# Two expert weight pieces loaded into the upper half of the gate buffer, before the output products of a hybrid decoder layer

## The chip, the cores and the metric

The kernel runs on one core of one Trainium2 chip. The metric is the device time of one execution in microseconds. TensorE is PE in the rows, VectorE DVE, ScalarE ACT, GpSimd POOL, and SyncE, which issues most of the transfers, SP.

## What is computed

One step of a one-layer hybrid decoder: 512 prompt tokens and 64 sample tokens, 1024 channels. A state-space branch and a sparse attention branch each give 1024 channels. They are multiplied by gates, added, multiplied by `w_out` and added to the input. Behind that stands a mixture of experts with 32 experts in 4 groups, two experts for a token. Cut to what matters here:

```python
gates = sigmoid(g_mrg)                      # 2 x 1024 channels, one half for each branch
merged = gate_ssm * ssm_out + gate_attn * attn_out
x = x + merged @ w_out
h = rms_norm(x, g_ffn)
g_sel = argmax(h @ w_router_group + b_router_group)
top_v, top_i = top_k(e_logits[g_sel], 2)    # h @ w_router_expert + b_router_expert
for block, e in blocks_of_tokens_by_expert:
    out[block] = (silu(h[block] @ w_exp_gate[e]) * (h[block] @ w_exp_up[e])) @ w_exp_down[e]
y = rms_norm(x + weighted sum of a token's two rows of out, g_final)
```

## The kernel before, in words

Everything is float32. The program is written by hand, engine by engine, with semaphores; no scheduler moves anything. It has five phases, and the last, `tail`, joins `merge` (branches, output product, router), `experts` and `combine`. Each engine runs its three parts one behind the other.

**The buffers.** `c.arena` is one tensor of on-chip memory that the phases cut up again and again with `Region`. In `merge`, `sig` (line 1565) holds 16 tiles of 128 channels by 576 tokens from `AT_Z4` on: tiles 0 to 7 are the gates of the state-space branch, tiles 8 to 15 those of the attention branch. Behind `sig` lie `g_ffn`, `w_route`, `b_route`, and the row buffer `X_rows` with its tables. The attention products are multiplied into tiles 8 to 15 (line 1881). The state-space products are multiplied into tiles 0 to 7 (line 1909), and tiles 8 to 15 are added to them (line 1910, semaphore `proj_done`, 16 steps). The output product (line 1779) reads tiles 0 to 7 alone, so tiles 8 to 15 are dead from `proj_done` 16 on.

**The weights of the experts.** An expert has six pieces of 1 MB (`w_exp[b, p]`): four of gate and up weights, two of down weights. `c.sets` (line 1595) has three sets of six places, all of them over buffers of `merge` that are dead by the time. Expert b uses set b modulo 3. Set 1's pieces 2 to 5 lie over `sig`, as does set 2's piece 4, which also reaches into `g_ffn`.

**The order of the transfers.** SP issues them in the order of the program, and waits block all that stands behind:

```python
        sp.wait_ge(proj_ps, 16)
        for s, p in ((0, 3), (0, 4), (0, 5), (1, 0), (1, 1)):
            piece(s, p)
        for i in range(TILES - 1):
            sp.wait_ge(h_ready, i + 1)
            sp.dma_start(c.d["h"][...], h[...]).then_inc(h_stored, 16)
            sp.wait_ge(h_stored, 16 * (i + 1))
        sp.wait_ge(out_ps, 2 * TILES)
        for s, p in ((1, 2), (1, 3), (1, 4), (1, 5), (2, 0), (2, 1), (2, 2), (2, 3)):
            piece(s, p)
        sp.wait_ge(h_ready, TILES)
        piece(2, 4)
```

Behind it, in `experts`, line 2108 refills a place when TensorE has used its piece (`gu_used`, line 2107, and `down_used`, line 2112). The last piece of expert 2, line 2119, waits until the router's tables and weights are done.

**Router and first rows.** DVE forms h tile by tile (`normed`, line 1928, `h_ready`), SP writes it to memory (line 1668), and POOL writes the last tile (line 1682). PE turns h over (line 1761) and forms the logits with `w_route` (line 1769); DVE chooses the experts (`choose`, line 1931 on; the last mask, line 1965, is `m_ready`). PE ranks the tokens (lines 1798 to 1801), DVE and PE find the tokens of the first two experts (lines 1992 and 1808), and POOL gathers their rows of h from memory into `X_rows` by two indirect transfers (line 1688). PE begins expert 0 with the transposes of the gathered rows (line 2186), then gate and up products (line 2199, each half gives back two places), then the full tables (line 1816), for which DVE has worked in the meantime (lines 2019 to 2031).

Of the kernel before, what the change touches and what calls it, by code (L numbers as in the profile page):

```python
# [28 lines left out]
P = 128  # L29
# [4 lines left out]
TOK = SEQ + NB * NT  # L34
HALF = TOK // 2
TILES = 5
# [132 lines left out]
AT_Z4 = 4992  # L169
# [1386 lines left out]
def merge(nc, c):  # L1556


    def sem(name):
        return c.sem("merge_" + name)  # L1560
# [3 lines left out]
    small = Region(c.arena, AT_Z4 + 16 * TOK, AT_KT)  # L1564
# [14 lines left out]
    g_ffn = small.take([P, D])  # L1579
    w_route = small.take([P, KD, 36])  # L1580
    b_route = small.take([P, 36])
    c.X_rows = small.take([SLOTS, 2, D])
    c.table = small.take([SLOTS, TABLE, 2], I32)
    c.blocks = small.take([1, BLOCKS + 3], I32)
    c.token = small.take([SLOTS, 2, 1], I32)
    at_z = Region(c.arena, AT_Z4, AT_Z4 + 5 * 2048)
    at_out = Region(c.arena, AT_KT, AT_XM)
    at_attn = Region(c.arena, AT_X2_END, AT_LOCAL)
    at_glu = Region(local, 3072, 3072 + 6 * 2048)
    over_z = [at_z.take([P, 4, 512]) for _ in range(5)]  # L1590
    over_out = [at_out.take([P, 4, 512]) for _ in range(4)]
    over_attn = [at_attn.take([P, 4, 512]) for _ in range(2)]
    over_glu = [at_glu.take([P, 4, 512]) for _ in range(6)]
    over_w1 = Region(c.arena, c.w1_at, c.w1_at + 2048).take([P, 4, 512])
    c.sets = [[over_w1] + over_attn + over_glu[0:3], over_glu[3:5] + over_z[0:4], over_out + [over_z[4], over_glu[5]]]

    ss = route.take([P, TILES])
    lg = route.take([P, TILES, 36])
# [23 lines left out]
    glu_ps, glu_tanh, glu_done, proj_ps, proj_done, out_ps, x_done = (  # L1622
        sem("glu_ps"), sem("glu_tanh"), sem("glu_done"), sem("proj_ps"), sem("proj_done"), sem("out_ps"),
        sem("x_done"))
    sq2, h_ready, h_stored, ht_ps, ht_out, lg_ps = (
        sem("sq2"), sem("h_ready"), sem("h_stored"), sem("ht_ps"), sem("ht_out"), sem("lg_ps"))
    ge_ready, ge_exp, te_ready, te_exp, m_ready, rank_ps, pick_ready, table_ps = (
        sem("ge_ready"), sem("ge_exp"), sem("te_ready"), sem("te_exp"), sem("m_ready"), sem("rank_ps"),
        sem("pick_ready"), sem("table_ps"))
# [13 lines left out]
    def sync(sp):  # L1643
        sp.dma_start(w_attn[:], c.d["w_attn"]).then_inc(wa_in, 16)
        sp.dma_start(sig[:, 8:16], c.d["sig"][8:16].rearrange("m p t -> p m t")).then_inc(gate_a_in, 16)
        sp.dma_start(w_glu[:], c.d["w_glu"]).then_inc(wg_in, 16)
        sp.dma_start(w_ssm[:], c.d["w_ssm"]).then_inc(ws_in, 16)
        sp.dma_start(sig[:, 0:8], c.d["sig"][0:8].rearrange("m p t -> p m t")).then_inc(sig_in, 16)
        sp.dma_start(g_ffn[:], c.d["g_ffn"]).then_inc(rt_in, 16)
        sp.dma_start(w_route[:], c.d["w_route"]).then_inc(rt_in, 16)  # L1650
        sp.dma_start(b_route[:], c.d["b_route"]).then_inc(rt_in, 16)
        def piece(s, p):
            sp.dma_start(c.sets[s][p], c.d["w_exp"][s, p]).then_inc(c.piece_in[s][p], 16)

        piece(0, 0)
        sp.wait_ge(y_ps, NY)
        sp.dma_start(w_out[:], c.d["w_out"]).then_inc(wo_in, 16)
        sp.wait_ge(attn_ps, 16)
        sp.dma_start(x[:, 0:4], c.d["x"][0:SEQ].rearrange("(i p) d -> p i d", p=P)).then_inc(x_in, 16)
        sp.dma_start(x[0:64, 4], c.d["x"][SEQ:TOK]).then_inc(x_in, 16)  # L1660
        piece(0, 1)
        piece(0, 2)
        sp.wait_ge(proj_ps, 16)
        for s, p in ((0, 3), (0, 4), (0, 5), (1, 0), (1, 1)):
            piece(s, p)
        for i in range(TILES - 1):
            sp.wait_ge(h_ready, i + 1)
            sp.dma_start(c.d["h"][i * P:i * P + ROWS[i]], h[0:ROWS[i], i % 2]).then_inc(h_stored, 16)
            sp.wait_ge(h_stored, 16 * (i + 1))
        sp.wait_ge(out_ps, 2 * TILES)  # L1670
        for s, p in ((1, 2), (1, 3), (1, 4), (1, 5), (2, 0), (2, 1), (2, 2), (2, 3)):
            piece(s, p)
        sp.wait_ge(h_ready, TILES)
        piece(2, 4)

    def gpsimd(pool):
# [190 lines left out]
    def vector(dve):  # L1867
# [188 lines left out]
        dve.wait_ge(c.weights_ready, 1)  # L2056

    return sync, gpsimd, tensor, table_tensor, scalar, vector


# [318 lines left out]
def tail(nc, c):  # L2379

    with ExitStack() as ctx:
        c.tail_local = local_tensor(nc, ctx, "tail")
        merge_sync, merge_gpsimd, merge_tensor, table_tensor, merge_scalar, merge_vector = merge(nc, c)
        experts_sync, experts_gpsimd, experts_tensor, experts_scalar, experts_vector = experts(nc, c, table_tensor)
        combine_sync, combine_scalar, combine_vector = combine(nc, c)
# [192 lines left out]
```

## Time and profile before

| | us |
|---|---|
| median of 3 runs | 1260.64 (1260.14 to 1262.17) |
| the profiled execution, its own time | 1264.99 |
| its span | 1263.3 |
| busy in the span: PE | 1041.9 |
| busy in the span: DVE | 410.2 |
| busy in the span: ACT | 328.0 |
| busy in the span: POOL | 251.9 |

Busy time of an engine is the time in which it has an instruction under way. The profiled execution is 4.35 us above the median, and its span, from the first to the last instruction, is 1.7 us shorter than its own time. Transfers are busy by 16 engines that all queues share, and their share is the mean over these. Times in the trace are counted from the start of the span.

### The profile page before, as it was taken

The numbers are of one execution on the slowest core, as the hardware profiler recorded it, in microseconds if no ns is written. First come the engines' busy times: TensorE is split into PE (matmuls) and PEld (weight loads), VectorE is DVE, ScalarE is ACT, GpSimd is POOL, SyncE is SP. The second block draws the span as 40 slices with busy tenths as digits, with TensorE's granted clock in tenths as the row PEclk, the third lists the DMA queues.
The fourth block names the chain that finished last, engine by engine and source line by source line (L and its number), as shares of the span: only waits on it lengthen the run. The fifth ranks groups of instructions, "written<-read, shape, count | busy, mean of one in ns | idle before, by whom it ended". The sixth has DMA issues, their size and how long they took to land.

```text
span 1263.3 us, 17373 instructions
## 1 busy us (share of the span) xinstructions
PE 1041.9 (82%) x6707; PEld 662.2 (52%) x6707; DVE 410.2 (32%) x917; ACT 328.0 (26%) x666; POOL 251.9 (20%) x551
## 2 busy tenths in 40 slices
PE   5999999779987776989999589987877788888870
PEld 5999999656665553767644333333332333333320
DVE  4346536646844443422413520100000000000006
ACT  6432221445642222120011112322222122211222
POOL 0005960388832110000000001111110111111010
PEclk9999999887978887989999679999899999998895
DMA  8322334331017542770220869999999999999956
GB/s 341 138 68 70 108 120 163 104 149 34 2 38 255 181 134 90 315 275 1 76 123 17 322 254 402 390 401 415 403 405 398 406 402 403 405 407 410 405 228 229
DMA packets 74993, 299.64 MB, mean 237 GB/s; under 512 B 12471, under 2 KB 34871, under 8 KB 48407
## 3 DMA queue, kind: packets, MB, share of 16 engines
q1 hardware_dynamic: 65854, 279.89, 57.5%
q0 software_dynamic: 7904, 17.59, 4.3%
q8 instruction: 53, 0.87, 0.3%
q10 hardware_dynamic: 1152, 1.05, 0.3%
q14 instruction: 30, 0.24, 0.1%
HBM read 284.26 MB, written 25.05 MB: 245 GB/s over the span
## 4 chain that ended last, share of the span: by engine, by line
DMA 27%; PE 25%; DVE 3%; issue 2%; SPq 2%; ACT 1%; POOL 0%; POOLq 0%
DMA local_tail<-in_w_exp 14%; DMA arena<-in_w_exp 11%; PE ps L2199 6%; PE ps L1779 5%; PE ps L1739 3%; PE ps L1700 3%; PE ps L1749 2%; PE ps L2216 2%; SPq L2108 1%; PE ps L2186 1%; PE ps L1716 1%; DVE arena L2358 1%; PE ps L1711 1%; SPq L2113 1%; DMA arena<-scratch_h,arena 1%
## 5 line engine op out<-in xcount | busy, mean ns | idle before, releaser
L352 PE MATMUL ps<-local_project 128*128 128x288 f32 (+4 forms) x1608 | 207.2, 291 | 15.3 <-DVE local_project L490 11.6
L2199 PE MATMUL ps<-arena,local_tail 128*64 128x512 f32 x760 | 196.7, 607 | 27.7 <-DMA arena<-in_w_exp 20.3
L352 PEld LDWEIGHTS ps<-local_project 128*128 128x128 f32 (+1 forms) x1608 | 205.8, 185 | 16.3 <-DVE local_project L391 11.5
L2301 DVE SCALAR_TENSOR_TENSOR local_tail<-arena,ps 64x512 f32<-64x512 f32 x32 | 21.7, 679 | 427.4 <-ACT arena L2267 427.4
L2199 PEld LDWEIGHTS ps<-arena,local_tail 128*64 128x64 f32 x760 | 63.2, 139 | 133.7 <-issue 132.1
L2216 PE MATMUL ps<-arena 128*64 128x512 f32 x256 | 89.3, 679 | 32.4 <-DMA arena<-in_w_exp 15.6
L2144 POOL DMA_INDIRECT scratch_rows<-local_tail,arena x32 | 29.5, 922 | 394.3 <-ACT local_tail L2275 393.2
L2216 PE MATMUL ps<-local_tail,arena 128*64 128x512 f32 x256 | 89.6, 681 | 16.1 <-DMA local_tail<-in_w_exp 16.1
L2199 PE MATMUL ps<-local_tail 128*64 128x512 f32 x264 | 80.1, 596 | 5.3 <-DMA local_tail<-in_w_exp 4.2
L2275 ACT ACTIVATE local_tail<-ps 64x512 f32<-64x512 f32 x64 | 37.9, 593 | 148.4 <-PE ps L2216 147.6
L2216 PEld LDWEIGHTS ps<-arena 128*64 128x64 f32 x256 | 26.4, 155 | 76.9 <-issue 73.5
L1779 PE MATMUL ps<-arena 128*128 128x512 f32 x128 | 57.4, 609 | 1.0 <-DVE arena L1910 1.0
L391 DVE TENSOR_TENSOR local_project<-arena,local_project 128x2048 fp32r<-128x2048 f32 (+1 forms) x15 | 35.6, 2372 | 66.6 <-ACT local_project L302 66.6
L2267 ACT ACTIVATE arena<-ps 64x512 f32<-64x512 f32 x32 | 18.9, 592 | 131.8 <-PE ps L2199 131.8
L2216 PEld LDWEIGHTS ps<-local_tail,arena 128*64 128x64 f32 x256 | 26.6, 155 | 39.4 <-issue 39.2
L2186 PEld LDWEIGHTS ps<-arena 64*128 64x128 f32 x297 | 24.7, 159 | 34.3 <-issue 26.0
L1269 PE MATMUL ps<-local_attention,arena 128*128 128x128 f32 x256 | 34.6, 298 | 9.0 <-DMA local_attention<-in_cache 7.5
L1779 PEld LDWEIGHTS ps<-arena 128*128 128x128 f32 x128 | 24.7, 195 | 31.8 <-issue 30.3
L2263 ACT ACTIVATE arena<-ps 128x256 f32<-128x256 f32 x32 | 12.3, 384 | 110.3 <-PE ps L2186 110.2
L2199 PEld LDWEIGHTS ps<-local_tail 128*64 128x64 f32 x264 | 24.7, 136 | 29.6 <-issue 28.1
L1269 PEld LDWEIGHTS ps<-local_attention,arena 128*128 128x128 f32 x256 | 33.0, 211 | 10.1 <-DMA local_attention<-in_cache 7.9
L2140 POOL DMA_INDIRECT arena<-scratch_h,arena x32 | 30.0, 938 | 30.7 <-DVE arena L2035 20.8
(401 smaller groups left out, 1505.7 us busy)
## 6 DMA issues: line engine op xcount, KB each, us to landing
arena<-in_w_exp SPq DMA_DIRECT2D x127, 1024.0 KB, 29.0
local_tail<-in_w_exp SPq DMA_DIRECT2D x65, 1024.0 KB, 29.4
arena<-in_w_rest SPq DMA_DIRECT2D x9, 1024.0 KB, 5.6
local_attention<-in_cache SPq DMA_DIRECT2D x56, 128.0 KB, 2.7
arena<-in_w_wide SPq DMA_DIRECT2D x6, 1040.0 KB, 4.9
arena<-scratch_sig SPq DMA_DIRECT2D x2, 2304.0 KB, 13.4
arena<-in_x SPq DMA_DIRECT2D x2, 2048.0 KB, 11.7
arena<-in_cache SPq DMA_DIRECT2D x32, 128.0 KB, 2.2
```

Source lines behind the costliest of these rows:

```text
L352: mm = pe.matmul(out, stationary(s, k), moving(m, k), start=k == 0 and a == 0, stop=k == KD - 1 and a == 2)
L391: dve.tensor_tensor(W[:, n % 2, 1, :, 0:width], raw[:, n % 2, :, 0:width], W[:, n % 2, 0, :, 0:width].bitcast(F32), ALU.subtract).then_inc ...
L1269: mm = pe.matmul(c.ps[:, 5, quarter * P:(quarter + 1) * P], c.w1[:, s, j], mov, start=j == 0, stop=j == 7)
L1700: mm = pe.matmul(c.ps[:, 6 + u % 2, 0:HALF], w_attn[:, k, m * P:(m + 1) * P], c.aT[:, k, t], start=k == 0, stop=k == 3)
L1739: mm = pe.matmul(c.ps[:, 2 * e + u % 2, 0:HALF], w_glu[:, k, (4 * e + j) * P:(4 * e + j + 1) * P], yT[:, k, t], start=k == 0, stop=k == 3)
L1779: mm = pe.matmul(c.ps[:, n, :], sig[:, k, i * P:(i + 1) * P], w_out[:, k, n * 512:(n + 1) * 512], start=k == 0, stop=k == KD - 1)
L2140: pool.indirect_dma_start(X[:, q], None, c.d["h"], bass.IndirectOffsetOnAxis(ap=at.bitcast(U32), axis=0), bounds_check=TOK - 1, oob_is_err ...
L2144: pool.indirect_dma_start(c.d["rows"], bass.IndirectOffsetOnAxis(ap=at.bitcast(U32), axis=0), Y[:, q], None, bounds_check=2 * TOK - 1, oob ...
L2186: return pe.transpose(out, rows, ident) if k else pe.matmul(out, rows, ident, start=True, stop=True)
L2199: mm = pe.matmul(c.ps[SLOTS * u:SLOTS * (u + 1), BANKS[q][u], :], XT[:, 4 * half + k], c.sets[s][2 * half + u][:, k], start=half == 0 and ...
L2216: mm = pe.matmul(c.ps[SLOTS * h:SLOTS * (h + 1), 6 + h, :], HT[:, k], c.sets[s][4 + h][:, k], start=k == 0, stop=k == KE - 1)
L2275: act.activation(Y[:, q, h * 512:(h + 1) * 512], c.ps[SLOTS * h:SLOTS * (h + 1), 6 + h, :], ACT.Copy).then_inc(y_out, 1)
```

## The change

Two pieces of the second expert's weights (set 1, pieces 2 and 3) get places over tiles 8 to 15 of `sig`, and SP issues them when `proj_done` stands at 16, ahead of the stores of h. Pieces 4 and 5 of set 1 now lie over tiles 0 to 7 and still wait for the output product. Set 2's piece 4 now reaches over `w_route` and `b_route` too, and waits for `m_ready` in place of the fifth `h_ready`. `X_rows` and what lies behind it move up by 188 floats (from 15556 to 15744).

```diff
@@ merge, places
     b_route = small.take([P, 36])
+    at_half = AT_Z4 + 8 * TOK
+    at_tail = at_half + 2 * 2048
+    small.pos = max(small.pos, at_tail + 2048)
     c.X_rows = small.take([SLOTS, 2, D])
...
-    at_z = Region(c.arena, AT_Z4, AT_Z4 + 5 * 2048)
+    at_low, at_high = Region(c.arena, AT_Z4, at_half), Region(c.arena, at_half, at_tail + 2048)
...
-    over_z = [at_z.take([P, 4, 512]) for _ in range(5)]
+    over_low = [at_low.take([P, 4, 512]) for _ in range(2)]
+    over_high = [at_high.take([P, 4, 512]) for _ in range(3)]
...
-    c.sets = [[over_w1] + over_attn + over_glu[0:3], over_glu[3:5] + over_z[0:4], over_out + [over_z[4], over_glu[5]]]
+    c.sets = [[over_w1] + over_attn + over_glu[0:3], over_glu[3:5] + over_high[0:2] + over_low, over_out + [over_high[2], over_glu[5]]]
@@ merge, sync
         for s, p in ((0, 3), (0, 4), (0, 5), (1, 0), (1, 1)):
             piece(s, p)
+        sp.wait_ge(proj_done, 16)
+        piece(1, 2)
+        piece(1, 3)
         for i in range(TILES - 1):
...
         sp.wait_ge(out_ps, 2 * TILES)
-        for s, p in ((1, 2), (1, 3), (1, 4), (1, 5), (2, 0), (2, 1), (2, 2), (2, 3)):
+        for s, p in ((1, 4), (1, 5), (2, 0), (2, 1), (2, 2), (2, 3)):
             piece(s, p)
-        sp.wait_ge(h_ready, TILES)
+        sp.wait_ge(m_ready, 1)
         piece(2, 4)
```

The order of SP's transfers around the change, before. Row 421 is the first of the five pieces that wait for `proj_ps`, rows 423 and 424 are the stores of h, and rows 425 to 427 the nine pieces behind the output product. The names of semaphores are those of their first user in the program, since they are used again.

```order
421 L1653 DMA local_tail<-in_w_exp 128x2048 [waits project_chan_tanh]
422 L1653 DMA local_tail<-in_w_exp 128x2048 x4
423 L1668 DMA scratch_h<-local_tail 128x1024 [waits project_mean_ready]
424 L1668 DMA scratch_h<-local_tail 128x1024 [waits project_mean_ready,project_root_done] x3
425 L1653 DMA arena<-in_w_exp 128x2048 [waits project_roped,project_root_done]
426 L1653 DMA arena<-in_w_exp 128x2048 x7
427 L1653 DMA arena<-in_w_exp 128x2048 [waits project_mean_ready]
428 L2108 DMA arena<-in_w_exp 128x2048 [waits experts_gu_used] x3
```

And now:

```order
421 L1657 DMA local_tail<-in_w_exp 128x2048 [waits project_chan_tanh]
422 L1657 DMA local_tail<-in_w_exp 128x2048 x4
423 L1657 DMA arena<-in_w_exp 128x2048 [waits project_gates_tanh]
424 L1657 DMA arena<-in_w_exp 128x2048
425 L1675 DMA scratch_h<-local_tail 128x1024 [waits project_mean_ready]
426 L1675 DMA scratch_h<-local_tail 128x1024 [waits project_mean_ready,project_root_done] x3
427 L1657 DMA arena<-in_w_exp 128x2048 [waits project_roped,project_root_done]
428 L1657 DMA arena<-in_w_exp 128x2048 x5
429 L1657 DMA arena<-in_w_exp 128x2048 [waits sample_ot_out]
430 L2115 DMA arena<-in_w_exp 128x2048 [waits experts_gu_used] x3
```

Two of the eight pieces behind the output product moved ahead of the four stores of h, with a wait of their own, and the ninth piece has another wait. Nothing else in SP's order and nothing in the order of PE, DVE, ACT and POOL is different.

## Rows read from the trace of the kernel before

**Rows 1.** The page: the chain that ended last, by engine and by line.
```profile
DMA 27%; PE 25%; DVE 3%; issue 2%; SPq 2%; ACT 1%; POOL 0%; POOLq 0%
DMA local_tail<-in_w_exp 14%; DMA arena<-in_w_exp 11%; PE ps L2199 6%; PE ps L1779 5%; PE ps L1739 3%; PE ps L1700 3%; PE ps L1749 2%; PE ps L2216 2%; SPq L2108 1%; PE ps L2186 1%; PE ps L1716 1%; DVE arena L2358 1%; PE ps L1711 1%; SPq L2113 1%; DMA arena<-scratch_h,arena 1%
```
**Rows 2.** Windows; behind the stretch: busy us by engine, granted clock, DMA share, GB/s.
```profile
core 0: us, PE busy (x) PEld busy (x) DVE busy (x) ACT busy (x) POOL busy (x), PEclk, DMA share, GB/s
702.00:728.00 26.00, 8.68 (x62) 7.79 (x60) 18.03 (x64) 3.72 (x8) 2.76 (x4) 0.56 0.97 384
728.00:738.00 10.00, 8.55 (x31) 3.42 (x33) 1.20 (x3) 0.60 (x1) 0.00 (x0) 0.60 0.00 1
738.00:748.00 10.00, 9.23 (x57) 4.17 (x53) 3.83 (x17) 1.78 (x3) 1.86 (x2) 1.00 1.01 398
...
760.00:1200.00 440.00, 363.95 (x1761) 143.68 (x1759) 38.12 (x56) 95.62 (x172) 52.94 (x57) 0.95 1.02 404
```
**Rows 3.** Timeline of SP: start, us until the last issue ended, line, count.
```profile
624.31 2.59 SPq L1653 DMA_DIRECT2D local_tail<-in_w_exp  x5
644.29 50.18 SPq L1668 DMA_DIRECT2D scratch_h<-local_tail  x4
701.44 5.41 SPq L1653 DMA_DIRECT2D arena<-in_w_exp  x9
737.09 3.76 SPq L2108 DMA_DIRECT2D arena<-in_w_exp  x3
...
748.01 0.33 SPq L2119 DMA_DIRECT2D local_tail<-in_w_exp  x1
```
**Rows 4.** The chain that ended last, in order of time, 720 to 744 us.
```profile
720.73 7.99 DMA arena<-scratch_h,arena
...
728.76 1.45 PE ps L2186 x9
...
730.88 9.61 PE ps L2199 x32
740.50 0.80 PE ps L2186 x9
741.29 2.37 PE ps L1816 x20
```
**Rows 5.** Windows of 1 us at the end of the nine pieces.
```profile
726.00:727.00 1.00, 0.00 (x0) 0.00 (x0) 0.93 (x3) 0.00 (x0) 0.00 (x0) 0.50 0.92 283
727.00:728.00 1.00, 0.00 (x0) 0.00 (x0) 0.90 (x4) 0.00 (x0) 0.00 (x0) 0.50 0.46 127
```
**Rows 6.** DMA issues (x, us to landing): second gather (722 to 724), loop's last (1205 to 1215); a window.
```profile
arena<-scratch_h,arena POOLq DMA_INDIRECT x1, 6.3
...
arena<-scratch_h,arena POOLq DMA_INDIRECT x1, 6.1
...
1212.50:1215.00 2.50, 2.07 (x13) 0.89 (x11) 0.00 (x0) 0.38 (x1) 0.00 (x0) 1.00 0.72 293
```
**Rows 7.** The last scatter, in the chain; its window; DMA issues of all gathers, 760 to 1200.
```profile
1230.84 3.10 DMA scratch_rows<-local_tail,arena
...
1230.00:1232.50 2.50, 0.00 (x0) 0.00 (x0) 0.00 (x0) 0.02 (x1) 1.44 (x4) 0.69 0.10 23
...
arena<-scratch_h,arena POOLq DMA_INDIRECT x28, 8.0
```
**Rows 8.** Windows of 5 us during and behind the five pieces.
```profile
630.00:635.00 5.00, 5.00 (x13) 2.22 (x12) 0.69 (x1) 0.00 (x0) 0.00 (x0) 1.00 1.01 421
...
640.00:645.00 5.00, 5.00 (x13) 2.28 (x12) 1.65 (x4) 2.64 (x4) 0.00 (x0) 1.00 0.00 0
```
**Rows 9.** Timeline of DVE: the last gated sum, the last mask, the last step before the tables.
```profile
624.81 0.46 DVE L1910 TENSOR_TENSOR arena<-arena 128x288 f32<-128x288 f32 x1
...
714.97 0.26 DVE L1965 TENSOR_TENSOR local_tail<-local_tail 128x96 f32<-128x96 f32 x1
...
728.77 0.49 DVE L2031 TENSOR_TENSOR local_tail<-arena,local_tail 128x320 f32<-128x320 f32 x1
```

## The prediction

> **What bounds the kernel now.** I read the page's chain first. Waits for expert weights are 25% of the span [rows 1], so the long stage of the experts is bound by transfers, not by TensorE. The windows date it: from 738 us to 1200 us the DMA engines show a share of 1.01 or 1.02, at 398 GB/s at its beginning and 404 behind it [rows 2]. A stage like that ends earlier by as much as it starts earlier, or by the bytes that are taken out of it. Here no byte is taken out. The same windows show that the moved pieces belong to an earlier burst: it runs from 702 to 728 us (share 0.97), and then the engines rest for 10 us, share 0.00, until 738. All three sets are full by then, and SP has nothing to issue until TensorE gives back the first place, at 737.09 [rows 3]. So moving 2.10 MB out of the burst does not of itself bring the saturated stage forward. It only makes the rest longer, unless something in the chain waits for the burst.
>
> Something does. The chain in order of time [rows 4] shows what leads to 737.09. When DVE has found the first expert's tokens, POOL issues the gather of their rows, at 720.73, in the middle of the burst, and it takes 7.99 us to land. PE begins at 728.76, ACT copies, and the gate and up products start at 730.88; half of them give back the first place. The gather lands about 0.7 us after the burst is over: the traffic falls to 283 and 127 GB/s in the windows from 726 and 727 us [rows 5], and to nothing behind 728 [rows 2]. The second gather, issued 2.02 us later, takes 6.3 us [rows 6] and so lands at 729.05, 0.33 us after the first. Two requests 2 us apart that land together are held by a common thing, and the weights are what is there.
>
> **The change part by part.**
>
> *The two early pieces.* The five pieces before them are issued by 626.9 [rows 3], and `proj_done` reaches 16 at 625.27 (624.81 and 0.46 [rows 9]), so SP's new wait costs nothing; two more issues at 0.52 us each (2.59 for five) end near 628. At 421 GB/s [rows 8] five pieces of 1.05 MB take 12.5 us, to some 637.5, and two more 5.0, to some 642.5. The next on SP's queue is the first store of h, at 644.29 [rows 3], so it is not held. If it were, by a us or two, ACT needs that store only for the tile two further on, and the tiles are 17 us apart (four stores over 50.18 us [rows 3]). The output products go on meanwhile. Thirteen records in each 5 us with the engines at 421 GB/s, and thirteen with them at rest [rows 8]: weights that arrive cost PE nothing. Price 0.
>
> *The later burst, shorter.* Between 702 and 728 us 26.00 us times 384 GB/s is 9.98 MB: nine pieces (9.44), the last tile of h (0.26), and 0.28 of gathered rows. Without two pieces the weights and h are 7.60 MB. At the full rate, 0.42 MB in a us, two pieces less are 5.0 us less. The burst thins out from 726 [rows 5], so now it would from about 721 and be over by 723.
>
> *The ninth piece.* It now waits for `m_ready`, 715.23 (714.97 and 0.26 [rows 9]), where before it waited for h. At 715.23 nearly 1 MB of the other six is still on its way (6.55 MB at 0.42 from 702 last until 717.6), so the engines don't run dry and its bytes follow without a gap, to about 721. Behind it on SP stand only refills that wait for PE, at 732 or later. It is used by the down product of expert 2, some 40 us on. Price 0.
>
> *The gather.* It is issued at 720.73 as before, since the route to it (DVE, PE, POOL) is not touched. It now meets the last 0 to 1 us of the burst. How long it takes at rest no gather of this trace shows. The nearest row is the last scatter, the same queue and up to 64 rows of 4 KB as well, with the engines at a share of 0.10: 3.10 us [rows 7]. The far bound is the loop's last gather, 6.1 us beside the thinning end of the weights (share 0.72) [rows 6]; full load gives 8.0 [rows 7]. I take 3.3 us, the scatter's and a little for what is left of the burst, because the engines are nearly empty then. Gain 7.99 − 3.3 = 4.7 us; by the bounds 4.9 and 1.9.
>
> The Trainium skill, "DMA: Bandwidth & Descriptors", section on queues, rings and completion order, says that each DMA engine takes turns between the queues, a packet at a time; by that a gather on POOL's own queue would hardly wait for SP's weights, with them or without, and the change would bring nothing. The trace goes against it: 7.99 us in the burst stand against 3.10 for the scatter at rest, and the gathers in the saturated stage take a median of 8.0 [rows 7].
>
> *Behind the gather.* PE's transposes (1.45 us), ACT's copy and the products (9.61) shift whole [rows 4]. The tables need DVE's last step, at 729.26 (728.77 and 0.49 [rows 9]); PE comes to them at 741.29 now and at 736.6 then, so DVE still is not the bound. Line 2119 waits for them at 748.01 [rows 3]; that shifts too. The refills start 4.7 us sooner and the saturated stage, and all behind it, with them.
>
> *The moved row buffer.* 188 floats further on; no row shows a cost of a start address. 0, with 1 us to either side over the 30 later gathers.
>
> Sum: −4.7 us. The profiled execution would have a span of 1258.6 and a time of 1260.3. It stands 4.35 above the median; on the median, 1260.64 − 4.7 = 1255.9.
>
> **The clock.** In the burst TensorE had little to do (8.68 us of 26) and was at 0.50 of its clock (1.2 GHz) at its end [rows 2, 5]. The mean of 0.60 from 728 to 738 [rows 2] is 8 us at 0.50 and 2 at 1.00 (2.4 GHz), so it rose near 736, 7.2 us after PE began expert 0 at 728.76 [rows 4]. The sum takes it that the rise comes equally late after the new start. Of the 9.61 us of products 5.1 were then at the low level, which cost 2.6 (half of it). Were the clock high at once, 2.6 more would be gained; that is the lower end of the range.
>
> **The rivals.**
>
> *The gather has its own pace* (same, or a small gain). The 7.99 us are latency of many small requests, not of the weights. For it: the saturated stage, where the queue is never short, has 8.0 as well, no more than this burst near its end, and the loop's last still took 6.1 when the load was already thin [rows 6, 7]. Against it: the common landing of the two gathers. At 6.1 us the gain is 1.9 (1258.7), at 7.99 nothing (1260.6).
>
> *Full credit for the bytes.* Someone who looks at the share of the stage expects 2.10 MB at 404 GB/s, 5.2 us (1255.4). The 10 us of rest speak against it as a mechanism, but it comes out near my number. The two are told apart by where SP's first refill stands and by how long the rest is.
>
> *The clock stays low through expert 0* (slower). Beginning 4.7 us earlier, PE comes to its work with another history. If the rise came only behind the tables, the products would take 14.1 us in place of 9.61, the transposes 1.6 for 0.80 and the tables 4.7 for 2.37 [rows 4]: 7.7 us more before line 2119, less the 4.7. The first four refills are used up by then and the others hang on that line, so the stage would go on 3.0 us later: 1263.6. It decides from 4.7 us of added low clock on. Against it: before, the rise came after 7.2 us of the same work.
>
> *Nothing is early.* SP could find the pieces blocked; but tiles 8 to 15 have no reader behind `proj_done`, and the order shows them ahead of the stores.
>
> **How the numbers follow.** A measurement of this kernel can tell about 0.2%, 2.5 us, from no change. The gather freed from the weights: 0.66 (with the full credit's number, which is within its range), 1253.3 to 1257.5. A gather of its own pace, in part or whole: 0.22, of which 0.04 still comes to over 2.5 us. The clock low for longer: 0.06, and 0.06 for a small loss or gain elsewhere, split evenly between same and faster. Faster 0.73, same 0.21, slower 0.06. The range must take in the case of 1.9 us to hold 8 in 10: 1253.3 to 1259.0.
>
> **What would show it.** Right: a rest of the engines between the early pieces and the first store of h of about 1 us; the first gather landing in 3 to 4 us, near 724; PE's line 2186 starting there; the first refill near 732.4, line 2119 near 743.3; and from 733 on the same windows as before at the same rate. Wrong: a gather that still takes 6 to 8 us, so that PE starts at 727 or later; or an early start whose gain is gone when the last weights land, which would mean that the saturated stage does not simply shift.

## The result, and the profile after

| | before | changed |
|---|---|---|
| median of 5 runs, us | 1262.17 | 1256.32 |
| lowest and highest | 1260.14 to 1266.16 | 1253.86 to 1256.92 |
| ratio, 95% interval | | 0.994 (0.9912 to 0.9968) |
| profiled execution: own time, span | 1264.99, 1263.3 | 1256.32, 1254.6 |

The medians are 5.85 us apart; the forecast was 4.7 us faster, 1255.9. (Two further runs of the kernel before moved its median from 1260.64 to 1262.17.) The interval of the ratio leaves 1 out, so the changed kernel is faster. The lines of the changed file have moved: 1653 is now 1657, 1668 is 1675, 1779 is 1786, 2186 is 2193, 2199 is 2206, 2108 is 2115 and 2119 is 2126.

The timeline of SP, beside [rows 3]:

```profile
621.59 2.62 SPq L1657 DMA_DIRECT2D local_tail<-in_w_exp  x5
624.25 0.97 SPq L1657 DMA_DIRECT2D arena<-in_w_exp  x2
641.57 50.18 SPq L1675 DMA_DIRECT2D scratch_h<-local_tail  x4
698.72 14.14 SPq L1657 DMA_DIRECT2D arena<-in_w_exp  x7
728.68 3.76 SPq L2115 DMA_DIRECT2D arena<-in_w_exp  x3
...
739.60 0.33 SPq L2126 DMA_DIRECT2D local_tail<-in_w_exp  x1
```

The whole stretch stands 2.72 us earlier than before, and that is not the change's: the tail phase itself begins 2.73 us earlier, at its first transfer:

```profile
493.93 0.33 SPq L1648 DMA_DIRECT2D arena<-in_w_attn  x1
```

Before, that line stood at 496.66. So all comparisons below are made from the issue of the five pieces, 624.31 before and 621.59 here. From there the first store of h is at 19.98 in both, so the early pieces held up nothing; the first refill is at 107.09 in place of 112.78, and line 2126 at 118.01 in place of 123.70. From that line to the end of the span are 515.0 us, against 515.3 before. The difference of the spans, 8.7 us, is thus 2.7 from ahead of the change, 5.7 from it and 0.3 behind it. From here on a time "from the five pieces" is counted from that issue in the same trace.

The chain that ended last, beside [rows 4] (start, us, what):

```profile
718.01 3.38 DMA arena<-scratch_h,arena
...
721.43 1.45 PE ps L2193 x9
722.90 0.60 ACT local_tail L2266
...
723.55 8.53 PE ps L2206 x26
732.08 0.81 PE ps L2193 x9
732.88 2.37 PE ps L1823 x20
```

The gather is issued at 96.42 us from the five pieces in both traces, and lands in 3.38 us in place of 7.99: 4.61 of the 5.69. The other 1.08 is in the products, 8.53 in place of 9.61. The windows, with the columns of [rows 2], show why for both:

```profile
702.00:718.00 16.00, 7.45 (x50) 6.67 (x50) 10.16 (x41) 2.37 (x5) 0.56 (x1) 0.52 1.01 419
718.00:729.00 11.00, 6.88 (x29) 3.04 (x31) 7.89 (x22) 0.60 (x1) 2.20 (x3) 0.61 0.13 41
718.00:719.00 1.00, 0.00 (x0) 0.00 (x0) 0.93 (x3) 0.00 (x0) 0.99 (x1) 0.50 0.38 156
...
726.00:727.00 1.00, 1.00 (x6) 0.38 (x4) 0.51 (x2) 0.00 (x0) 0.00 (x0) 0.75 0.00 0
...
760.00:1200.00 440.00, 366.36 (x1744) 145.39 (x1740) 37.30 (x55) 94.30 (x169) 53.49 (x60) 0.94 1.02 404
```

The burst is all but over at 718, when the gather is issued: in the next us the share is 0.38. The engines then rest until 729, but for the gathers. The saturated stage (760 to 1200) runs at 404 GB/s as before. The clock rises in the middle of the window from 726, 3.0 us into the products; before, it was 5.1 us.

### The profile page after: what moved, and what is told of

Same layout as the page of the kernel before. It is cut to its first block, busy times and chain, and to the rows that moved or that the text cites. A ratio compares the mean times of both kernels' runs of the same rounds, so it can differ in the third digit from the quotient of the medians.

```text
span 1254.6 us, 17373 instructions
## 1 busy us (share of the span) xinstructions
PE 1045.9 (83%) x6707; PEld 666.1 (53%) x6707; DVE 411.0 (33%) x917; ACT 327.5 (26%) x666; POOL 251.3 (20%) x551
## 4 chain that ended last, share of the span: by engine, by line
PE 27%; DMA 25%; DVE 3%; issue 2%; SPq 2%; ACT 1%; POOL 0%; POOLq 0%; DVEq 0%
DMA local_tail<-in_w_exp 15%; DMA arena<-in_w_exp 10%; PE ps L2206 7%; PE ps L1786 5%; PE ps L2223 3%; PE ps L1746 3%; PE ps L1707 3%; PE ps L1756 2%; PE ps L2193 1%; SPq L2120 1%; PE ps L1723 1%; SPq L2115 1%; DVE arena L2365 1%; PE ps L1718 1%; PE ps L1776 1%
## 5 line engine op out<-in xcount | busy, mean ns | idle before, releaser
L2223 PE MATMUL ps<-arena 128*64 128x512 f32 x256 | 92.9, 697 | 34.6 <-DMA arena<-in_w_exp 17.0
L2223 PE MATMUL ps<-local_tail,arena 128*64 128x512 f32 x256 | 93.1, 698 | 14.8 <-DMA local_tail<-in_w_exp 14.8
```

Of the source, the lines that this page charges most:

```text
L2223: mm = pe.matmul(c.ps[SLOTS * h:SLOTS * (h + 1), 6 + h, :], HT[:, k], c.sets[s][4 + h][:, k], start=k == 0, stop=k == KE - 1)
```

## The experiments

**Two theories stood against each other.** A: the first gather was slowed by the weights, and only what stands between it and the first refill matters. (A refill is a transfer of line 2108, or 2115, into a place that TensorE has given back.) B: two pieces' traffic, 5.2 us of the saturated rate, was moved to where it is free. Third, C: the gather has its own pace, and the gain is from the places.

**e0_after and e4_after, the changed kernel again.** No edit.

> The changed kernel once more, beside the kernel before on the same chip. Both theories (the gather freed from the weights; or two pieces' worth of traffic saved) give 4.7 to 6 us less than before, a ratio of 0.995 to 0.996. What tells is the part outside the change: the traces so far show the tail phase of the changed kernel starting 2.7 us sooner, ahead of anything that was changed. If that is chance from execution to execution, the start of the tail phase (first issue of w_attn) will lie anywhere between 493 and 497 us here, and the distance from the output product to the end stays 6 us under that of before.

> The changed kernel as the measure for the three beside it on this chip. Its gather takes 3.3 to 3.6 us again. Its two executions so far raised TensorE's clock 2.9 and 3.0 us into the first expert's products, where the kernels with a full burst took 5.1 to 5.5: if that belongs to the change, it is under 3.5 us here again; if it is chance, it may be anything from 1 to 6 us.

Medians 1255.45 against 1262.12 for before (0.9949, 0.9931 to 0.9968) and 1257.57 against 1263.15 (0.995, 0.993 to 0.9969). The gathers took 3.42 and 3.41 us. The tail phase began at 491.20 in the first, 5.5 us ahead of that of before, with the same code up to there. It differs that much from execution to execution, about as much as the change is worth. The clock rose 2.9 us into the products both times, as it had 3.0 us: with the changed order this repeats.

**e1_hold3, the gather freed with no early piece.** In the kernel before:

```diff
-        for s, p in ((1, 2), (1, 3), (1, 4), (1, 5), (2, 0), (2, 1), (2, 2), (2, 3)):
+        for s, p in ((1, 2), (1, 3), (1, 4), (1, 5), (2, 0), (2, 1)):
             piece(s, p)
         sp.wait_ge(h_ready, TILES)
+        sp.wait_ge(c.rows_in[0], 16)
+        piece(2, 2)
+        piece(2, 3)
         piece(2, 4)
```

> The kernel before with no early piece at all: the last three pieces of set 2 are held on SP until the first gathered rows have landed. If the gather was held by the weights, it meets 6 pieces instead of 9, lands in 3.1 to 3.5 us in place of 7.99, PE begins expert 0 some 4.6 us sooner, the three held pieces (7.5 us) fit in the rest before the first refill, and the time falls by 4.5 to 6 us, as in the changed kernel. If the gain is the two pieces' bytes moved to an idle time before the output products, nothing is moved here and the time is that of before, within 1 us; holding the pieces may even cost up to 1 us. If the gather has its own pace, no gain either, and a gather of 6 to 8 us.

1258.58 against 1262.12, 0.9962 (0.9945 to 0.9979). Its chain:

```profile
716.31 3.64 DMA arena<-scratch_h,arena
...
719.99 1.45 PE ps L2189 x9
721.47 0.61 ACT local_tail L2262
...
722.11 10.02 PE ps L2202 x32
```

B falls: nothing was moved ahead of the output products, and most of the gain is there: by the traces 3.9 of 5.7 us at the wait of line 2126 (here 2122), by the ratios 4.8 of 6.4 and by the medians 3.5 of 6.7 against e0_after. The gather freed 4.35 us. The products took 10.02 us, with a clock that rose only at 728.0 (windows):

```profile
727.00:728.00 1.00, 1.00 (x4) 0.24 (x2) 0.00 (x0) 0.00 (x0) 0.00 (x0) 0.50 1.02 434
728.00:729.00 1.00, 1.00 (x8) 0.32 (x6) 0.00 (x0) 0.00 (x0) 0.00 (x0) 0.97 0.93 393
```

So the first refill came at 108.85 us from the five pieces (728.73 less 619.88), 1.76 behind the changed kernel's. Holding the three pieces cost nothing behind it: from line 2122 to the end are 515.0 us, as in the changed kernel. The medians are 3.5 us apart, a little less than A expected; the ratio stands for 4.8.

**e2_places_only, the new places with the old order.** In the changed kernel:

```diff
-        sp.wait_ge(proj_done, 16)
-        piece(1, 2)
-        piece(1, 3)
...
-        for s, p in ((1, 4), (1, 5), (2, 0), (2, 1), (2, 2), (2, 3)):
+        for s, p in ((1, 2), (1, 3), (1, 4), (1, 5), (2, 0), (2, 1), (2, 2), (2, 3)):
```

> The changed kernel with its new places (row buffer 188 floats on, set 1 over the upper half, the last piece behind the last mask), but all pieces issued in the order of before. If the order alone makes the gain, the time is that of before within 1.5 us and the gather takes 7 to 8.5 us again. If the places (the start address of the row buffer) carry part of the gain, it is that much faster than before with the gathers of the saturated stage under a median of 8.0 us. If the later wait of the ninth piece costs or gives, it shows as a gather off 8 us.

1262.39 against 1262.12, 1.0006 (0.9987 to 1.0026). Gather and products are those of before:

```profile
720.19 7.85 DMA arena<-scratch_h,arena
...
730.20 9.81 PE ps L2203 x32
```

By the time, which can tell some 2.5 us, and by the trace (first refill at 112.82 us from the five pieces, against 112.78), the places, the moved row buffer and the wait for `m_ready` are worth nothing by themselves. C falls.

**e3_reload2, early pieces and a full burst.** In the changed kernel, with expert 0's waits for the two pieces raised by 16:

```diff
         sp.wait_ge(out_ps, 2 * TILES)
-        for s, p in ((1, 4), (1, 5), (2, 0), (2, 1), (2, 2), (2, 3)):
+        for s, p in ((0, 1), (0, 2), (1, 4), (1, 5), (2, 0), (2, 1), (2, 2), (2, 3)):
```

> The changed kernel with the burst filled up again: two pieces of expert 0 that are long there are loaded a second time at its head, so the early pieces stay early but the gather meets as much traffic as before. If the gather is what the change frees, it takes 7 to 8.5 us again, the first refill comes back to where it was, and the gain is gone: the time of before within 1.5 us. If having set 1's pieces early is worth something of itself, 4 to 5 us of gain are left.

1263.27 against 1262.12, 1.0016 (0.9997 to 1.0035).

```profile
718.70 7.83 DMA arena<-scratch_h,arena
...
728.69 9.70 PE ps L2206 x32
```

The pieces were as early as in the changed kernel, and the gain was gone with the short gather. Together with e1_hold3 this shows A from both sides. What it is in the weights' transfers that makes the gather wait, the runs do not show.

**e5_hold7, how much can be held.** In the changed kernel, `sp.wait_ge(c.rows_in[0], 16)` ahead of all seven pieces, and no wait for `m_ready`.

> The changed kernel with all seven pieces behind the output product held until the first rows have landed. The gather then meets nothing and should take 3.0 to 3.3 us. If traffic is free only as long as it fits in the rest before the first refill (7.3 us here), the 17.5 us of seven pieces overrun it by 10, the refills queue behind them, and the kernel is 8 to 10 us slower than the changed one, about 1264, though PE starts expert 0 as early. If all that counts is when PE starts, the time is that of the changed kernel within 1 us.

1266.76 against 1257.57 for the changed kernel measured beside it, 9.2 us slower; 1.0035 (1.0013 to 1.0057) to before. The gather, SP's timeline and the windows:

```profile
717.67 3.40 DMA arena<-scratch_h,arena
...
721.14 3.54 SPq L1657 DMA_DIRECT2D arena<-in_w_exp  x7
728.51 3.76 SPq L2115 DMA_DIRECT2D arena<-in_w_exp  x3
```
```profile
703.00:721.00 18.00, 7.32 (x50) 6.55 (x50) 12.07 (x49) 2.37 (x5) 2.76 (x4) 0.50 0.10 24
...
729.00:740.00 11.00, 9.65 (x59) 4.31 (x55) 4.42 (x17) 1.78 (x3) 1.86 (x2) 1.00 1.01 424
```

PE asks for its first refill as early as in the changed kernel (107.26 us from the five pieces, against 107.09), but the engines still carry held pieces, and the time is lost behind the router: from line 2126 to the end are 524.2 us in place of 515.0. Seven pieces at 0.42 MB in a us are 17.5 us, and the rest after the landing was 7.4 (721.11 to 728.51), so 10.1 would have been over; 9.2 were lost. Bytes that fit in the rest of the engines cost nothing, as in e1_hold3, and what is beyond it costs nearly its full time. The run also gives the gather's time at rest, with a share of 0.10 around it: 3.40 us. So the 3.38 of the changed kernel had nothing left to gain from less traffic.

**e6_warm, e7_warm_last and e8_warm_again, TensorE kept at work.** In the changed kernel, with a=5, b=11, d=7 (e7_warm_last: 0, 0, 7). The products of constants go to a bank that nobody reads then; no result depends on them.

```diff
+        def warm(n):
+            for _ in range(n):
+                pe.matmul(c.ps[:, 4, 0:256], c.k("ident"), c.K[:, 0:256], start=True, stop=True)
...
         logits(LAST - 1)
+        warm(a)
         turn(LAST)
         logits(LAST)
+        warm(b)
         pe.wait_ge(m_ready, 1)
...
             mm.then_inc(first_ps, 1)
+        warm(d)
```

> The changed kernel with products of constants, whose result nothing reads, put on TensorE where it waits between the output product and the first expert: 5 ahead of the last turn, 11 ahead of the last mask, 7 ahead of the first rows. If the low clock at the start of expert 0 is what is left on the path to the first refill, the clock stays at 1.00 through, the first products take 7.1 to 7.2 us in place of 8.5, the transposes 0.8 in place of 1.45, and the kernel is 2 to 3 us faster than the changed one, 1252 to 1254. If the clock falls all the same, the fillers run at 0.50 and hold up the ranks by some 3 us: 3 us slower. If the first refill is not what sets the saturated stage, no change.

> The changed kernel with only the last 7 of these fillers, right ahead of the first rows. They run at the low clock, 0.85 us each or 6 us, so they may end 2 us behind the landing of the gather and delay the start of expert 0 by that much; the clock should then rise within the first 2 us of the products. Sum between 1 us faster and 2 us slower than the changed kernel. If the delay shows and the clock does not rise sooner, 2 us slower.

> The changed kernel with its 23 fillers once more, beside the other two: again some 3 us under the changed kernel, a ratio of 0.992 to 0.995 to the kernel before, the first products in 7.1 us.

e6_warm: 1254.51 against 1257.57 for the changed kernel, 3.1 us less; 0.9935 (0.9912 to 0.9957) to before. Its chain:

```profile
715.14 3.83 DMA arena<-scratch_h,arena
...
719.01 0.89 PE ps L2200 x9
719.92 0.61 ACT local_tail L2273
...
720.57 7.09 PE ps L2213 x27
```

The wait of line 2126 (here 2133) came at 114.91 us from the five pieces (735.17 less 620.26), 3.10 ahead of the changed kernel's 118.01. The clock did not stay up throughout, against the expectation, but it stood at 1.00 for the transposes and the products. The gather was issued 1.54 us sooner (94.88 for 96.42), since the steps ahead of it ran faster, and then landed in 3.83. Why 0.4 more than in the changed kernel is open: the burst had 2.5 us left at its issue, but e9_hold3_warm below has the same 3.83 with the burst over.

e7_warm_last: 1256.73 against 1257.57, no difference that can be told; its line came at 118.30, 0.29 behind the changed kernel's. The fillers ran at the low clock and held the transposes up by 2.36 us; behind them the clock was up, and transposes and products took 2.07 less. Both halves are about what was expected.

e8_warm_again gave the median 1254.17 against 1264.68 (0.9929, 0.9904 to 0.9955), but its profiled execution missed what I expected of the products:

```profile
712.87 5.11 DMA arena<-scratch_h,arena
...
719.58 8.78 PE ps L2213 x32
```

The fillers were done 1.4 us before the rows were there, and the clock fell to 0.50 at the start of the products. Its line came at 117.89, hardly ahead of the changed kernel's 118.01, where e6_warm, the same kernel, had 114.91. Gather and burst were issued at the same distance from the five pieces in both; why the gather took 1.3 us longer is open.

**e9_hold3_warm and e10_before_warm, the two causes apart.** The same fillers in e1_hold3, and in the kernel before (with 12 at the last place).

> The kernel before with three pieces held back behind the first rows, as e1_hold3, and the 23 fillers. e1_hold3 had the short gather, but its clock rose 5.9 us into the products and its first refill came 1.8 us later than in the changed kernel. If the clock was all that set it apart, the fillers bring both to the same time: within 1 us of the changed kernel with fillers, a ratio of 0.992 to 0.995. If loading early pieces is worth something beyond the gather, or holding costs something, 2 us or more slower.

> The kernel before with fillers alone (5, 11 and 12). The gather stays at 7.5 to 8.5 us; only the clock is helped: transposes 0.6 us and products up to 2.6 us shorter, so 2 to 3 us faster than before, a ratio of 0.9975 to 0.9985. If the fillers end behind the gather, up to 2 us of that is lost. If gather and clock were one and the same thing, it would gain as much as the changed kernel with fillers, 7 us or more.

e9_hold3_warm: 1255.46, 0.9934 (0.9908 to 0.996), beside 1254.17 for e8_warm_again, 1.3 us apart where 1 was expected, but far within the intervals. Its first refill stands at 103.99 us, e6_warm's at 104.00; e8_warm_again's, with the clock low, at 106.97. Where the clock is up in both, holding and loading early are the same, so these traces show nothing but the clock that set e1_hold3 apart. e10_before_warm: 1256.82 against 1264.68, 0.9938 (0.9915 to 0.9961). This is 7.9 us by the medians and missed by a factor of two or more, on the good side. Its chain:

```profile
716.55 7.25 DMA arena<-scratch_h,arena
...
723.85 0.88 PE ps L2193 x9
724.75 0.61 ACT local_tail L2266
...
725.40 7.09 PE ps L2206 x31
```

Its line 2126 (2119 before) is at 118.34 from the five pieces, 5.36 sooner than before. (The ratio's interval is 4.9 to 10.7 us, so the 5.36 lies within it; the rest of the 7.9 no trace places.) I had counted the transposes (0.57) and the products (2.52). Further 1.55 are upstream: the gather was issued at 94.87 for 96.42. The ranks, in the chain of before and of this run:

```profile
715.29 0.90 PE ps L1798 x2
716.19 0.68 PE ps L1800 x2
716.87 0.28 PE ps L1801 x2
```
```profile
712.27 0.27 PE ps L1804 x2
712.55 0.27 PE ps L1806 x2
712.82 0.15 PE ps L1807 x2
```

They took 0.69 us at a clock of 1.00 in place of 1.86 at 0.50, and began 0.39 sooner. (The last mask was there 1.19 sooner, since turn and logits were faster too, but the fillers held PE for 0.86 of it.) The last 0.74 is that the gather took 7.25 in place of 7.99. That is no clock of TensorE, and no run shows its cause. The sum is 5.38, and 4.6 of it is the low clock ahead of the first refill: it cost this kernel as much as the slow gather (4.61). In the traces the early pieces give 5.7 from before, the fillers 5.4, and both together 8.8 in e6_warm and 5.8 in e8_warm_again. The 8.8 is 2.3 less than the sum: 1.08 of the clock stands in both terms, the 0.74 of the slow gather is gone with the slow gather, and e6_warm's gather was 0.45 longer than the changed kernel's.

The gather of e10_before_warm also landed at 723.80, while the weights were still on their way:

```profile
724.00:725.00 1.00, 0.72 (x9) 0.58 (x9) 0.93 (x3) 0.25 (x1) 0.00 (x0) 1.00 0.98 274
```

So a gather issued well inside the burst takes 7 to 8 us, but it does not wait for the last of the weights.

**The best version** is the changed kernel with fillers: 1254.51 beside 1257.57 and 1263.15, and 1254.17 beside 1264.68 in another comparison. Against the changed kernel alone the gain was timed once side by side, and the intervals of the two ratios (0.9912 to 0.9957 and 0.993 to 0.9969) overlap.

## Why the prediction was right, and where it was off

*What bounds the kernel.* Right: the saturated stage kept its 404 GB/s and its length (515.0 and 515.3 us from line 2119 on) and moved as a whole. Over all traces but e5_hold7's this length is 514.3 to 518.1, so this stage by itself can move the end by more than 3 us from one execution to another, whatever the kernel. Right too that the bytes were worth nothing (e3_reload2) and that the rest of the engines only grew.

*The early pieces, price 0.* Right: the first store of h stands at 19.98 us from the five pieces in both traces, and the traffic was over just ahead of it:

```profile
640.00:641.00 1.00, 1.00 (x4) 0.44 (x3) 0.91 (x2) 0.02 (x1) 0.00 (x0) 1.00 0.54 221
641.00:642.00 1.00, 1.00 (x3) 0.38 (x2) 0.54 (x1) 0.00 (x0) 0.00 (x0) 1.00 0.06 25
```

*The shorter burst.* I expected it over between 721 and 723; counted on that scale (2.72 more than in the new trace) it thinned out from 720.7 and was over by some 721.5. Part of the ragged end of the old burst may have been the gathers' own 0.27 MB. The miss cost nothing.

*The gather, 3.3 us.* Measured 3.38, 3.42 and 3.41, and 3.40 at rest. The last scatter was the right row to take it from. The prediction drew from the Trainium skill ("DMA: Bandwidth & Descriptors", on queues, rings and completion order), where each DMA engine takes turns between the queues by packets, that a gather on its own queue would hardly wait for the weights. Four executions with a full burst (7.99, 7.85, 7.83 and, with an earlier issue, 7.25) go against what was drawn from it; whether the engines take turns is not tested by them. The argument from the common landing, 0.33 us apart, was weaker than it looked: with a full burst the two gathers landed 1.3 us apart in e2_places_only, 1.7 in e3_reload2 and 2.6 in e10_before_warm. The conclusion holds by e1_hold3 and e3_reload2, not by that row.

*The clock.* This is the term that was mis-sized. The sum let it rise as late after the new start as before; it rose 2.1 us earlier within the products, 3.0 for 5.1, and gave 1.08 us. Less the 0.08 by which the gather fell short of 4.7, that is the 1.0 by which the trace's gain, 5.7, is over the forecast. I had it only as the end of the range (2.6 more). Why it rose earlier is open, as said below. e10_before_warm shows that I also looked at too short a stretch: with the transposes and what the low clock cost ahead of the gather it was 4.6 us, not 2.6.

*The number.* That 1255.9 stands within 0.5 us of 1256.32 is in part luck. It was counted from a median that two more runs moved up by 1.5 us, and the gain was 1.2 larger than forecast (5.85 for 4.7); the two nearly cancel.

*The rivals.* The gather's own pace was excluded by e1_hold3 and e5_hold7. Full credit for the bytes named 5.2 us, as near to the measured gain of 5.85 as mine or nearer, and was wrong: its mechanism fell in e1_hold3 and e3_reload2. The clock that stays low through the tables did not show in any kernel; e1_hold3 came nearest, with 10.02 us of products.

## What to carry to other kernels

Where prefetches run in a burst, look for the small latency-bound transfer that falls into it, on whichever queue: here 1 MB pieces that nobody needed yet made a small gather take 8 us instead of 3.4, and everything hung on the gather. Prefetch traffic is free only as long as it fits into the idle time of the engines ahead of the point where they become the bound; that idle time, not the share of the stage, says what may be moved or held. And when short dependent steps run on TensorE between two dense stages, read the granted clock over them too: here it stood at 0.50 from 706 to 736 us, and that cost as much as the slow gather.

## What was not expected

The clock rose 3.0, 2.9 and 2.9 us into the first products in three executions of the changed kernel (3.2 in e5_hold7), 5.1, 5.5 and 5.3 us with the full burst (before, e2_places_only, e3_reload2), and 5.9 in e1_hold3, whose products began only 0.27 us later (102.23 us from the five pieces, for 101.96). That kernel had held pieces on their way at the time, too. Nor is it enough that TensorE is at work. In e7_warm_last it was busy without a gap at 0.50 for 8 us, and in e6_warm the clock fell to 0.50 near 715.1, when it had been busy without a gap from 713 on (from 711 to 713, about 0.6 of the time):

```profile
718.00:726.00 8.00, 8.00 (x33) 6.86 (x34) 7.31 (x25) 0.00 (x0) 2.20 (x3) 0.50 0.53 208
```
```profile
714.00:715.00 1.00, 1.00 (x5) 0.90 (x6) 0.86 (x6) 0.00 (x0) 0.00 (x0) 1.00 0.97 410
715.00:716.00 1.00, 1.00 (x4) 0.80 (x4) 0.90 (x4) 0.00 (x0) 0.86 (x1) 0.57 0.95 401
```

Why the rise falls on one side or the other these runs don't settle; whoever shifts such a stage by a few us should expect one or two more or less from this alone.

The start of the tail phase varied from 489.3 to 496.7 us between executions, with the same code up to there: a comparison of two single traces needs a common point just ahead of the change.
